# Two blocks of two layers on one core: the norm between the blocks moved behind the first index products, and the first block's attention maxima moved ahead of two rotations

## The chip, the cores and the metric

One core of a Trainium2 chip runs the whole program. The metric is the device time in microseconds (us) of one execution, the median of several. The engines are TensorE (PE in the rows; PEld is its weight load), VectorE (DVE), ScalarE (ACT), GpSimd (POOL) and SyncE (SP), which each work through a list of their own in order and wait for one another on semaphores.

## What is computed

512 tokens of width 1024 pass through two layers of a first block and two layers of a second, all in float32:

```
# first block, each of its two layers; then rmsnorm(x, g_final)
h = rmsnorm(x, g_mix);  z = h @ w_in            # q, k, v, retention q/k/v/g, two gates
ya = sliding_window_sink_attention(aq, ak, av, sinks) @ w_a     # window 128, blocks of 128
yb = (norm(chunkwise_retention(rq, rk, rv)) * silu(rg)) @ w_b
x = x + (sigmoid(ga) * ya + sigmoid(gb) * yb) @ w_out
x = x + square(relu(rmsnorm(x, g_mlp) @ w_up)) @ w_down
# second block, each of its two layers
proj = x @ w_in                                  # q, k, v, index q, index k, index weights, ...
dots = einsum('bqhd,bsd->bqhs', q_idx, k_idx) * IDX_DIM ** -0.5
score = einsum('bqhs,bqh->bqs', relu(dots), w_idx * IDX_HEADS ** -0.5)
top_val, top_idx = lax.top_k(score, topk)        # the keys that attention may see
x = layer_norm(DN_ALPHA * x + mixer(...));  x = layer_norm(DN_ALPHA * x + conv_ffn(x))
```

`rmsnorm(x, g)` is x times g times one factor for each token, the inverse root of the mean square over the 1024 features. Between the blocks stands `rmsnorm(x, g_final)`, whose result is the stream x of the second block.

## The kernel before

The stream lies transposed in SBUF: `X[:, k, :]` is feature tile k (128 features on the partitions) by 512 tokens, k from 0 to 7. A float32 product is made from three matmuls: every operand is split into a high part in TensorE's fast format (`x_hi`, `w_hi`, written by ScalarE) and a low part (`x_lo` by VectorE, `w_lo` by GpSimd, value minus high part), and high by high, high by low and low by high are added up in PSUM. `XH` and `XL` hold the parts of the operand.

Weights come in panels of 1 MB, in the order in which they are used. SyncE loads a panel into one of two `RAW` buffers when GpSimd has finished with the panel two before it; ScalarE's `hi(c)` (L1257, two instructions) writes its high part, GpSimd (L349, four instructions) its low part. A few panels, the two index panels of the second block's first layer among them, have high and low buffers of their own (`own_hi`, `own_lo`), so that `hi` doesn't wait for TensorE to be done with an older panel.

The order on each engine is the order of the code. Helpers are generators (`entry`, `gemm_rows`, `norm_squares`) that are advanced by hand inside other loops with `run(work, n)`, n steps at a time. `T.after`, `A.after`, `V.after` are the waits of TensorE, ScalarE and VectorE for named events, `done` names one.

Entry to a layer of the first block. TensorE multiplies `x * g_mix` without the token factor (`u_hi`, `u_lo`, VectorE L1997) while the squares of x are summed on VectorE (L1961, events `n1_acc`); `token_sums` (L660) reduces the sum over the partitions, ScalarE takes the root (L1537, `token_root`), VectorE the reciprocal (L1988, `n1_inverse`), and `spread` (L715) writes the factor to all partitions of PSUM bank 5. The factor goes into the rotation table (L2283) and, with `scale_again` (L2010, L1939), into a second pair XH/XL for the rest of the products. In layer 0 `start_clock` (L667) runs dummy matmuls ahead of the first products.

Attention of the first block (L740 on TensorE, L2062 on VectorE) runs in 8 steps of two pairs of heads; steps 0 and 1 use q tiles 0, 1 and 2, 3. TensorE's order is `scores(0)`, one piece of filler product (12 matmuls), `scores(1)`, filler, `scores(2)`. `scores(i)` (L746) writes PSUM banks 4 and 5 and waits for `roped 1` or `roped 3`, the rotation of its q tiles, and, from i = 1 on, for `s_read` of step i - 1, which is VectorE's `maxima(i - 1)` (L2055, a masked read of the scores with their minimum, L2060). VectorE's order ahead of it is `scale_again`, the rotations (`rope`, four instructions L1944 to L1950) of tiles 4, 1, 2, 3 (in layer 1: tiles 0, 1, 4 before `scale_again`, tiles 2 and 3 behind it), `maxima(0)`, `maxima(1)`. ScalarE loads the retention's rotation table into `ROT` once `roped 3` is there, and then starts the exponentials.

The feed-forward ends with eight tiles m added to X by VectorE (L2236); events `ffn_out k`. In its last part ScalarE calls `run(beside, 5)`, five steps of the next layer's entry, and then `hi` of the next panel, or of the next two where they have buffers of their own; VectorE runs one step of its own entry behind each addition from m = 2 on.

Between the blocks `inverse_deviation` (L719) on TensorE waits for the last squares, sums them, waits for the factor and spreads it, with dummy matmuls (`keep_clock`, L674) in the gaps; `norm` writes X scaled, `x_hi` and `x_lo`; then `gemm_two` multiplies the two index panels, 8 rows k of 12 matmuls of 384 columns into banks 0 to 3, and `gemm` the panel `misc` (index key, index weights).

Of the kernel before, what the change touches and what calls it, by code (L numbers as in the profile page):

```python
# [15 lines left out]
F32 = mybir.dt.float32  # L16
# [210 lines left out]
def program(nc, stream, x_in, consts_in, rot_in, vec_in, wgate_in, pos_in, out, marks):  # L227
    ctx = ExitStack()
    with ctx:
# [282 lines left out]
        def _(pe):  # L512
# [80 lines left out]
            def gemm_two(n, banks, ready, high_ready, name, columns):  # L593
# [7 lines left out]
                for k in range(KD):  # L601
# [5 lines left out]
                    for j, b in enumerate(banks):  # L607
                        c, p = (k * 2 + j % 2) * P, n + j // 2
                        mm = pe.matmul(PS[:, b, columns], high(p)[:, c:c + P], XL[:, k, columns], start=False, stop=(k == KD - 1))
                        if k == KD - 1:  # L610
                            T.done(mm, *name(j))
                marks[("panel", n)] = marks[("panel", n + 1)] = marks[name(3)]
# [105 lines left out]

            def inverse_deviation(bank, t, l, which):  # L719

                T.after((t, l, which + "_acc", KD - 2), bank_reader[bank], own=False)
                token_columns(TMP[:, 2, :], bank, P, True, False)
                T.after((t, l, which + "_sq", KD - 1), own=False)
                T.done(token_columns(TMP[:, (KD - 1) % 2, :], bank, P, False), t, l, which + "_ms")
                bank_reader[bank] = (t, l, which + "_root")
                keep_clock(bank + 1, 1)
                spread(bank + 1, (t, l, which + "_inverse"), (t, l, which + "_spread"))
                bank_reader[bank + 1] = (t, l, which + "_scaled", KD - 1)
                keep_clock(bank, 2)
# [241 lines left out]
            start_clock(5)  # L971
            for l in range(DEPTH):
# [11 lines left out]
                run(keys, 2)  # L984
# [98 lines left out]
            inverse_deviation(4, "f", 0, "n1")  # L1083

            for l in range(DEPTH):
# [4 lines left out]
                gemm_two(w["iq"], banks, h_ready, lambda k: (t, l, "x_hi", k), lambda m: (t, l, "q", 8 + m), columns_b(8))  # L1090
# [150 lines left out]
        def _(act):  # L1241
# [55 lines left out]
            def attention(pairs, l, t, fillers):  # L1297
# [31 lines left out]
                exponentials(0)  # L1329
                exponentials(1)  # L1330
# [202 lines left out]
            def token_root(bank, ready, name):  # L1533

                A.after(ready)
                sums = PS[:, bank, 0:S:P] if name[0] == "f" else PS[:, bank, 0:NB]
                A.done(act.activation(ST[:, 100:104], sums, ACT.Sqrt, scale=1.0 / D, bias=ST[:, 96:97]), *name)  # L1537

            def norm(t, l, which, squared, bank, second_panel, to_x=False):
# [1018 lines left out]
```

How the kernel before makes its waits and increments, by code:

```python
    def after(self, *names, own=True):  # L205
        need = {}
        for name in names:
            if name is None or (name not in self.marks and not self.marks.get("complete")):
                continue
            who, n = self.marks[name]
            need[who] = max(need.get(who, 0), n)
        if own:
            need[self.name] = self.n
        for who, n in need.items():
            if n > 0:
                self.eng.wait_ge(self.sems[who], n)
# [65 lines left out]
        def const_dma(eng, dst, src, name):  # L283
            if n_consts[0]:
                eng.wait_ge(const_loaded, 16 * n_consts[0])
            eng.dma_start(dst, src).then_inc(const_loaded, 16)
            n_consts[0] += 1
            marks[name] = ("const", 16 * n_consts[0])
# [27 lines left out]
        @block.sync  # L317
# [6 lines left out]
            sp.dma_start(RAW[:, 1, :], stream[1:2, :, :].rearrange("o p n -> p (o n)")).then_inc(raw_full[1], 16)
            with sp.Fori(1, NPANELS // 2) as i:
                for s in range(2):
                    sp.wait_ge(lo_ready, 2 * i + s + 1)
                    sp.dma_start(RAW[:, s, :], stream[bass.ds(2 * i + s, 1), :, :].rearrange("o p n -> p (o n)"))\
                        .then_inc(raw_full[s], 16)
            for k in range(KD):
                sp.wait_ge(sems["act"], marks.get(("b", DEPTH - 1, "ln2_x", k), ("act", 1))[1])
                sp.dma_start(out.rearrange("(k p) s -> p k s", p=P)[:, k, :], X[:, k, :]).then_inc(stored, 16)
            sp.wait_ge(stored, 16 * KD)
```

## Time and profile before

| | before |
|---|---|
| median of 3 executions | 3340.94 us (3340.58 to 3341.14) |
| the profiled execution: own time, span | 3339.35 us, 3337.5 us |
| TensorE matmul busy | 3301.5 us, 99% |
| VectorE, ScalarE, GpSimd busy | 1567.9, 1370.2, 1470.4 us |
| HBM read | 294.74 MB, 89 GB/s over the span |

The span is the stretch from the first to the last instruction of the profiled execution; 1.85 us of its own time lie around it. Times in the text below are us from the start of the span. "Busy" of a matmul is the modelled time from start to end; neighbours overlap, so the pace of TensorE is read from the distance of starts.

### The profile page before, as it was taken

How to read it: one execution, taken by the hardware profiler on the slowest of the kernel's cores; microseconds unless marked ns; L12 is line 12 of the kernel's file. 1: busy time of each engine (PE TensorE's matmuls, PEld its weight loads, DVE VectorE, ACT ScalarE, POOL GpSimd, SP SyncE). 2: the span in 40 equal slices, each digit the busy share in tenths (PEclk: the TensorE clock that was granted, in tenths of full speed). 3: DMA queues.
4: the chain of work that ended last, by engine and by line, in shares of the span. 5: the costliest groups of instructions: out<-in, count | busy, mean ns of one | idle time of the engine just before them, and what ended most of it. 6: DMA issues, size and time to landing. Idle time of an engine off the chain costs nothing. (4 is left out here: it accounts for less than half of the span.)

```text
span 3337.5 us, 45362 instructions
## 1 busy us (share of the span) xinstructions
PE 3301.5 (99%) x16670; PEld 2748.5 (82%) x16670; DVE 1567.9 (47%) x2488; ACT 1370.2 (41%) x1989; POOL 1470.4 (44%) x1102
## 2 busy tenths in 40 slices
PE   9999999999999999999999999999999999999998
PEld 7888888888788888888878888888887788888887
DVE  7523332226514442224973446544488625464445
ACT  5535332224635342223364453333343635443333
POOL 4433544445343444445433345445544233445453
PEclk9999999999999999999999999999999999999999
DMA  4222222222222322222211222222222121222221
GB/s 153 89 73 86 89 103 95 94 101 95 77 76 76 103 100 100 89 101 106 88 66 66 73 92 99 84 95 101 101 81 87 64 76 68 97 85 92 101 98 66
DMA packets 44014, 299.02 MB, mean 90 GB/s; under 512 B 4816, under 2 KB 5456, under 8 KB 8784
## 3 DMA queue, kind: packets, MB, share of 16 engines
q1 hardware_dynamic: 41696, 291.52, 24.5%
q10 hardware_dynamic: 2160, 5.33, 0.5%
q8 instruction: 107, 1.75, 0.2%
q14 instruction: 51, 0.42, 0.0%
HBM read 294.74 MB, written 2.10 MB: 89 GB/s over the span
## 5 line engine op out<-in xcount | busy, mean ns | idle before, releaser
L349 POOL TENSOR_TENSOR w_lo<-w_raw,w_hi 128x512 fp32r<-128x512 f32 x1024 | 1364.6, 1365 | 1778.2 <-ACT w_hi L1257 1778.2
L526 PE MATMUL ps<-x_hi,w_hi 128*128 128x512 f32 x2296 | 907.2, 395 | 3.1 <-DVE arena L2195 2.2
L528 PE MATMUL ps<-x_hi,w_lo 128*128 128x512 f32 x2296 | 894.8, 390 | 0.0
L527 PE MATMUL ps<-x_lo,w_hi 128*128 128x512 f32 x2296 | 894.1, 389 | 0.0
L1257 ACT ACTIVATE w_hi<-w_raw 128x1024 fp32r<-128x1024 f32 x516 | 515.9, 1049 | 463.0 <-PE ps L528 339.4
L526 PEld LDWEIGHTS ps<-x_hi,w_hi 128*128 128x128 f32 x2296 | 431.5, 188 | 100.3 <-issue 6.4
L528 PEld LDWEIGHTS ps<-x_hi,w_lo 128*128 128x128 f32 x2296 | 431.2, 188 | 91.2
L527 PEld LDWEIGHTS ps<-x_lo,w_hi 128*128 128x128 f32 x2296 | 431.6, 188 | 89.0 <-issue 2.2
L526 PE MATMUL ps<-y_hi,w_hi 128*128 128x512 f32 x1056 | 411.9, 390 | 2.2 <-issue 1.9
L528 PE MATMUL ps<-y_hi,w_lo 128*128 128x512 f32 x1056 | 410.9, 389 | 0.0
L527 PE MATMUL ps<-y_lo,w_hi 128*128 128x512 f32 x1056 | 410.8, 389 | 0.0
L2236 DVE TENSOR_TENSOR x<-x,ps 128x512 f32<-128x512 f32 x272 | 182.2, 684 | 255.5 <-PE ps L528 255.3
L2195 DVE SCALAR_TENSOR_TENSOR arena<-ps,vec,arena 128x511 f32<-128x511 f32 (+1 forms) x176 | 131.5, 749 | 300.4 <-ACT arena L1467 290.1
L526 PEld LDWEIGHTS ps<-y_hi,w_hi 128*128 128x128 f32 x1056 | 198.2, 188 | 45.1 <-issue 4.2
L527 PEld LDWEIGHTS ps<-y_lo,w_hi 128*128 128x128 f32 x1056 | 198.2, 188 | 41.5 <-issue 0.5
L528 PEld LDWEIGHTS ps<-y_hi,w_lo 128*128 128x128 f32 x1056 | 198.2, 188 | 41.3
L632 PE MATMUL ps<-w_hi,x_hi 128*128 128x256 f32 x768 | 222.2, 289 | 1.2 <-POOL w_lo L349 1.2
L633 PE MATMUL ps<-w_hi,x_lo 128*128 128x256 f32 x768 | 217.1, 283 | 0.0
L634 PE MATMUL ps<-w_lo,x_hi 128*128 128x256 f32 x768 | 217.1, 283 | 0.0
L1273 ACT ACTIVATE arena<-ps 128x512 f32<-128x512 f32 x136 | 81.3, 598 | 315.8 <-PE ps L528 240.6
L1467 ACT ACTIVATE arena<-ps,vec 128x512 f32<-128x512 f32 x88 | 68.4, 779 | 277.4 <-PE ps L528 277.4
L2206 DVE SCALAR_TENSOR_TENSOR arena<-ps,tmp 128x512 f32<-128x512 f32 x64 | 44.0, 691 | 238.5 <-PE ps L528 224.9
(269 smaller groups left out, 4178.7 us busy)
## 6 DMA issues: line engine op xcount, KB each, us to landing
w_raw<-stream SPq DMA_DIRECT2D x274, 1024.0 KB, 4.8
x<-x_t SPq DMA_DIRECT2D x4, 512.0 KB, 8.1
rotary<-rot ACTq DMA_DIRECT2D x4, 512.0 KB, 4.0
y_t<-x SPq DMA_DIRECT2D x8, 256.0 KB, 2.1
ct<-consts ACTq DMA_DIRECT2D x2, 770.0 KB, 4.4
arena<-pos ACTq DMA_DIRECT2D x2, 256.0 KB, 2.6
w_gate<-w_gate_in ACTq DMA_DIRECT2D x2, 256.0 KB, 2.8
vec<-vectors ACTq DMA_DIRECT2D x4, 116.0 KB, 2.0
```

Source lines behind the costliest of these rows:

```text
L349: ins = nc.gpsimd.tensor_tensor(low(c)[:, o:o + S], RAW[:, c % 2, o:o + S], high(c)[:, o:o + S].bitcast(F32), ALU.subtract)
L526: pe.matmul(ps, wh, xh, start=(k == 0), stop=False)
L527: pe.matmul(ps, wh, xl, start=False, stop=False)
L528: return pe.matmul(ps, wl, xh, start=False, stop=last)
L632: pe.matmul(ps, xh, wh, start=(k == 0), stop=False)
L633: pe.matmul(ps, xl, wh, start=False, stop=False)
L634: mm = pe.matmul(ps, xh, wl, start=False, stop=(k == KD - 1))
L1257: act.activation(wh[:, o:o + 2 * S], RAW[:, s, o:o + 2 * S], ACT.Copy)\
L1273: A.done(act.activation(dst, bank_of(*name), func, **kw), *(("read",) + name))
L1467: act.activation(AR[:, j, :], PS[:, j, :], ACT.Identity, scale=VEC[:, l % 2, bass.ds(tap, 1)], bias=VEC[:, l % 2, bass.ds(bias, 1)]).then_ ...
L2195: ins = dve.scalar_tensor_tensor(AR[:, j, tap:S], PS[:, j, 0:n], wv, AR[:, j, tap:S], ALU.mult, ALU.add)
L2236: dve.tensor_tensor(X[:, m, :], X[:, m, :], PS[:, 4 + m % 4, :], ALU.add).then_inc(down_added, 1)
```

## The change

Four edits.

1. `start_clock(5)` becomes `start_clock(8)`: eight dummy matmuls at the start in place of five.
2. In the entry to a layer of the first block TensorE runs one row of the key/value product between `token_sums` and `spread`, in place of two.
3. Attention of the first block: `maxima(0)` stands ahead of the rotations of q tiles 2 and 3, which stood ahead of it; on ScalarE the load of the second rotation table stands behind the first exponentials.
4. Between the blocks: the stream times `g_final`, without the token factor, is split (`u_hi`, `u_lo`, in a third entry generator, `last_entry`, which the last feed-forward advances), and the two index panels are multiplied with it. `token_sums` stands behind row 1, `spread` behind row 2. Index scores are relu of a product, so the positive factor of a query token can be put on the index weights: one more VectorE instruction there. The scaled stream X and its parts are written during rows 3 to 7 (`scale_stream`), each `x_hi k` when row k has been read. `inverse_deviation` and its dummy matmuls are gone.

```diff
-            start_clock(5)
+            start_clock(8)
...
-                run(keys, 2)
+                run(keys)
                 spread(5, (t, l, "n1_inverse"), (t, l, "n1_spread"))
...
-            inverse_deviation(4, "f", 0, "n1")
-
...
+                    index = gemm_two_rows(w["iq"], banks, lambda k: ("f", 0, "u_lo", k), lambda k: ("f", 0, "u_hi", k),
+                                          lambda m: (t, l, "q", 8 + m), columns_b(8), lambda k: ("f", 0, "u_read", k))
+                    run(index, 2)
+                    token_sums(TMP[:, 2, :], 4, ("f", 0, "n1_acc", KD - 1), ("f", 0, "n1_ms"))
+                    bank_reader[4] = ("f", 0, "n1_root")
+                    run(index)
+                    spread(5, ("f", 0, "n1_inverse"), ("f", 0, "n1_spread"))
...
# ScalarE
                 exponentials(0)
+                for _ in behind_first:
+                    pass
                 exponentials(1)
...
+            def last_entry():
+
+                x_ready = lambda k: ("a", DEPTH - 1, "ffn_out", k)
+                squared = norm_squares("f", 0, "n1", x_ready)
+                for k in range(KD):
+                    A.after(x_ready(k), "vec%d" % (DEPTH - 1))
+                    g = VB["g_final"] + k
+                    A.done(act.activation(XH[:, k, :], X[:, k, :], ACT.Copy, scale=VEC[:, 1, g:g + 1]), "f", 0, "u_hi", k)
+                    yield
+                    if k < 6:
+                        run(squared)
+                        yield
                 for _ in squared:
                     pass
                 warm_root()
-                token_root(bank, (t, l, which + "_ms"), (t, l, which + "_root"))
+                token_root(4, ("f", 0, "n1_ms"), ("f", 0, "n1_root"))
...
# VectorE
+            def last_entry():
+
+                adding = square_sums("f", 0, "n1")
+                for k in range(KD):
+                    g = VB["g_final"] + k
+                    V.after(("f", 0, "u_hi", k), "vec%d" % (DEPTH - 1), own=False)
+                    V.done(dve.scalar_tensor_tensor(XL[:, k, :], X[:, k, :], VEC[:, 1, g:g + 1],
+                                                    XH[:, k, :].bitcast(F32), ALU.mult, ALU.subtract), "f", 0, "u_lo", k)
+                    if k:
+                        run(adding)
+                    yield
...
                 maxima(0)
+                for _ in behind_first:
+                    pass
                 maxima(1)
...
-                for j in [j for j in (4, 1, 2, 3) if j not in early]:
+                for j in [j for j in (4, 1) if j not in early]:
                     rope(AR[:, j, :], SWAP_A, (t, l, "roped", j), [("read", t, l, "q", j)])
+
+                def last_ropes():
+                    for j in (2, 3):
+                        rope(AR[:, j, :], SWAP_A, (t, l, "roped", j), [("read", t, l, "q", j)])
+                        yield
...
+                if l == 0:
+                    V.done(dve.tensor_tensor(iw, iw, ST[:, 104:108].unsqueeze(2).broadcast_to([P, NB, 8]), ALU.mult))
```

How the edits stand in the lists of the engines. First VectorE at the start of the attention in layer 1 of the first block, before: the last of `scale_again`, the rotations of tiles 2 and 3 (the second is left out, it has the same four rows), then `maxima(0)`.

```order
L1939 TENSOR_TENSOR x_lo<-tmp,x_hi 128x512 x2
L1944 STREAM_SHUFFLE tmp<-arena 128x512
L1946 TENSOR_TENSOR tmp<-tmp,rotary 128x512
L1948 TENSOR_TENSOR arena<-arena,rotary 128x512
L1950 TENSOR_TENSOR arena<-arena,tmp 128x512
...
L2055 ISA tmp,stats<-ct,ps,stats 128x128
L2055 ISA stats 128x1
```

The same place in the changed kernel (its lines are numbered differently: 1939 is now 1961, 1944 to 1950 are 1966 to 1972, 2055 and 2060 are 2077 and 2082).

```order
L1961 TENSOR_TENSOR x_lo<-tmp,x_hi 128x512 x2
L2077 ISA tmp,stats<-ct,ps,stats 128x128
L2077 ISA stats 128x1
...
L2082 TENSOR_TENSOR stats<-stats 128x4
L1966 STREAM_SHUFFLE tmp<-arena 128x512
L1968 TENSOR_TENSOR tmp<-tmp,rotary 128x512
L1970 TENSOR_TENSOR arena<-arena,rotary 128x512
L1972 TENSOR_TENSOR arena<-arena,tmp 128x512
...
L2077 ISA tmp,stats<-ct,ps,stats 128x128
```

The first masked read of the scores has moved past both rotations; nothing else on VectorE has moved there. In layer 0 it is the same, with the rotations of tiles 4 and 1 ahead of `maxima(0)`.

Second, ScalarE at the end of the last feed-forward of the first block, before: high parts of the feed-forward's last panels and of the two index panels, then the eight squares and the root.

```order
L1257 ACTIVATE w_hi<-w_raw 128x1024 x6
L1257 ACTIVATE own_hi0<-w_raw 128x1024 x2
L1257 ACTIVATE own_hi1<-w_raw 128x1024 x2
L1282 ACTIVATE tmp<-x 128x512 x8
L1531 ACTIVATE stats<-stats 128x1
L1537 ACTIVATE stats<-ps,stats 128x4
```

The same place in the changed kernel (L1559 writes `u_hi`, L1289 a square).

```order
L1264 ACTIVATE w_hi<-w_raw 128x1024 x6
L1559 ACTIVATE x_hi<-x,vec 128x512
L1289 ACTIVATE tmp<-x 128x512
L1559 ACTIVATE x_hi<-x,vec 128x512
L1289 ACTIVATE tmp<-x 128x512
L1559 ACTIVATE x_hi<-x,vec 128x512
L1264 ACTIVATE own_hi0<-w_raw 128x1024 x2
L1264 ACTIVATE own_hi1<-w_raw 128x1024 x2
L1289 ACTIVATE tmp<-x 128x512
```

The high parts of both index panels have moved behind three `u_hi` and two squares.

Third, TensorE between the blocks, before: the last matmul of the feed-forward, the sums, dummies, spread, dummies, and the first index row.

```order
L528 MATMUL ps<-y_hi,w_lo 128x512
L679 MATMUL ps<-ct,tmp 128x128 x8
L674 MATMUL ps<-ct 128x256 x2
L715 MATMUL ps<-ct,stats 128x128 x4
L674 MATMUL ps<-ct 128x256 x4
L531 MATMUL ps<-x_hi,own_hi0 128x384
```

In the changed kernel the first index row follows the feed-forward's last matmul; this is the stretch from the end of index row 1 to the start of row 3 (row 2 is cut to its first two rows and its last).

```order
L613 MATMUL ps<-x_lo,own_hi1 128x384 x2
L668 MATMUL ps<-ct,tmp 128x1 x4
L531 MATMUL ps<-x_hi,own_hi0 128x384
L532 MATMUL ps<-x_hi,own_lo0 128x384
...
L613 MATMUL ps<-x_lo,own_hi1 128x384 x2
L723 MATMUL ps<-ct,stats 128x128 x4
L531 MATMUL ps<-x_hi,own_hi0 128x384
```

The sums and the spread now stand between rows of the index product, and the dummies are gone.

## Rows read from the trace of the kernel before

**Rows 1.** The page: busy time, and the clock granted to TensorE in 40 slices

```profile
PE 3301.5 (99%) x16670; PEld 2748.5 (82%) x16670; DVE 1567.9 (47%) x2488; ACT 1370.2 (41%) x1989; POOL 1470.4 (44%) x1102
PEclk9999999999999999999999999999999999999999
```

**Rows 2.** Waits of TensorE over the span: total, times, longest

```profile
PE ps L746 <- DVE stats L2055: 5.0, 2, 3.0
```

**Rows 3.** Timeline of TensorE at the start: start, duration, instruction, [idle before <- released by]

```profile
1.35 4.64 PE L667 MATMUL ps<-tmp 128*128 128x256 f32 x10 [1.35 <-DVE tmp L1935]
8.91 0.77 PE L531 MATMUL ps<-x_hi,w_hi 128*128 128x512 f32 x1 [2.92 <-ACT x_hi L1566]
...
14.15 0.39 PE L531 MATMUL ps<-x_hi,w_hi 128*128 128x512 f32 x1
...
28.25 1.05 PE L660 MATMUL ps<-ct,tmp 128*128 128x1 f32 x8 [0.29 <-DVE tmp L1961]
```

**Rows 4.** Timeline of VectorE at the start: six of the seven sums of squares

```profile
19.84 8.35 DVE L1961 TENSOR_TENSOR tmp<-tmp,scratch 128x512 f32<-128x512 f32 x6
```

**Rows 5.** Timeline of TensorE, start of the attention in layer 0

```profile
63.43 0.71 PE L746 MATMUL ps<-arena 64*128 64x128 f32 x8
...
70.05 0.81 PE L746 MATMUL ps<-arena 64*128 64x128 f32 x8 [2.95 <-DVE stats L2055]
```

**Rows 6.** Timeline of VectorE there: tile 1 from its shuffle, tiles 2 and 3, maxima

```profile
56.53 0.73 DVE L1944 STREAM_SHUFFLE tmp<-arena 128x512 f32<-128x512 f32 x1
...
59.57 0.75 DVE L1944 STREAM_SHUFFLE tmp<-arena 128x512 f32<-128x512 f32 x1
60.36 1.67 DVE L1946 TENSOR_TENSOR tmp<-tmp,rotary 128x512 f32<-128x512 f32 x1
...
67.87 0.69 DVE L1950 TENSOR_TENSOR arena<-arena,tmp 128x512 f32<-128x512 f32 x1
68.74 0.35 DVE L2055 CUSTOM_DVE_ANT_0 tmp<-ct,ps,stats 128x128 f32<-128x128 f32 x1 [0.18 <-DVE arena L1950]
...
69.94 0.16 DVE L2060 TENSOR_TENSOR stats<-stats 128x4 f32<-128x4 f32 x1
```

**Rows 7.** Timeline of GpSimd there: one panel's low part, and layer 1's

```profile
60.18 6.38 POOL L349 TENSOR_TENSOR w_lo<-w_raw,w_hi 128x512 fp32r<-128x512 f32 x4 [5.06 <-ACT w_hi L1257]
...
829.47 5.62 POOL L349 TENSOR_TENSOR w_lo<-w_raw,w_hi 128x512 fp32r<-128x512 f32 x4 [3.26 <-ACT w_hi L1257]
```

**Rows 8.** Timeline of TensorE, start of the attention in layer 1

```profile
827.27 0.71 PE L746 MATMUL ps<-arena 64*128 64x128 f32 x8
...
832.99 1.12 PE L746 MATMUL ps<-arena 64*128 64x128 f32 x8 [2.06 <-DVE stats L2055]
```

**Rows 9.** Timeline of VectorE there: the end of `scale_again`

```profile
820.96 2.40 DVE L1939 TENSOR_TENSOR x_lo<-tmp,x_hi 128x512 fp32r<-128x512 f32 x2 [0.21 <-ACT x_hi L1277]
```

**Rows 10.** Timeline of TensorE between the blocks: last matmul, first index row, `misc`

```profile
1550.28 0.39 PE L528 MATMUL ps<-y_hi,w_lo 128*128 128x512 f32 x1
...
1557.47 0.41 PE L531 MATMUL ps<-x_hi,own_hi 128*128 128x384 f32 x1
...
1574.46 0.47 PE L526 MATMUL ps<-x_hi,w_hi 128*128 128x512 f32 x1
```

**Rows 11.** Timeline of ScalarE: the high part of the second index panel

```profile
1540.11 2.01 ACT L1257 ACTIVATE own_hi<-w_raw 128x1024 fp32r<-128x1024 f32 x2 [7.21 <-DMA w_raw<-stream]
```

**Rows 12.** Timelines at the end of layer 0's feed-forward: ScalarE, GpSimd, TensorE, VectorE

```profile
768.61 0.72 ACT L1566 ACTIVATE x_hi<-x,vec 128x512 fp32r<-128x512 f32 x1 [1.27 <-DVE x L2236]
...
771.80 6.44 POOL L349 TENSOR_TENSOR w_lo<-w_raw,w_hi 128x512 fp32r<-128x512 f32 x4 [5.83 <-ACT w_hi L1257]
...
781.06 0.39 PE L528 MATMUL ps<-y_hi,w_lo 128*128 128x512 f32 x1
781.28 0.39 PE L531 MATMUL ps<-x_hi,w_hi 128*128 128x512 f32 x1
...
787.94 1.59 DVE L1961 TENSOR_TENSOR tmp<-tmp 128x512 f32<-128x512 f32 x1
```

More of the change, by code:

```diff
@@ L591, in gemm_rows, with gemm_two, gemm_two_rows @@
                 marks[("panel", n)] = marks[name(ms - 1)]
-            def gemm_two(n, banks, ready, high_ready, name, columns):
+            def gemm_two(*args):
+                for _ in gemm_two_rows(*args):
+                    pass
+            def gemm_two_rows(n, banks, ready, high_ready, name, columns, read=None):
                 for p in range(2):
@@ L611, in gemm_two @@
                             T.done(mm, *name(j))
+                        elif read and j == 3:
+                            T.done(mm, *read(k))
+                    if k < KD - 1:
+                        yield
                 marks[("panel", n)] = marks[("panel", n + 1)] = marks[name(3)]
@@ L717, in spread @@
                 T.done(mm, *name)
[L719 to L729, printed above, removed]
             def attention(pairs, l, t, fillers, ahead=0):
@@ L1591, in _ @@
             hi(0)
-            entries = [entry(l) for l in range(DEPTH)]
+            entries = [entry(l) for l in range(DEPTH)] + [last_entry()]
             for l in range(DEPTH):
@@ L1956, in sums @@
             def sums(src, ready, name):
-                for k in range(1, KD - 1 if name[0] == "f" else KD):
+                for k in range(1, KD):
                     a = src(0) if k == 1 else TMP[:, 2, :]
@@ L2003, in entry, with scale_stream @@
                     pass
+            def last_entry():
+                adding = square_sums("f", 0, "n1")
+                for k in range(KD):
+                    g = VB["g_final"] + k
[4 more added lines that the diff above has]
+                        run(adding)
+                    yield
+                for _ in adding:
+                    pass
+            def scale_stream(gain):
+                for k in range(KD + 1):
+                    if k < KD:
+                        V.after(("f", 0, "n1_spread"), own=False)
+                        V.done(dve.scalar_tensor_tensor(X[:, k, :], X[:, k, :], VEC[:, 1, gain + k:gain + k + 1],
+                                                        PS[:, 5, :], ALU.mult, ALU.mult), "f", 0, "n1_scaled", k)
+                    if k:
+                        j = k - 1
+                        lo(XL[:, j, :], X[:, j, :], XH[:, j, :], [("b", 0, "x_hi", j)], ("b", 0, "x_lo", j), own=False)
             def scale_again(t, l, gain):
@@ L2268, in ffn @@
                     pass
-            entries = [entry(l) for l in range(DEPTH)]
+            entries = [entry(l) for l in range(DEPTH)] + [last_entry()]
             for l in range(DEPTH):
```

77 lines of the change are left out of this document (34 added, 43 removed).

## The prediction

> **What bounds the kernel now.** I read the page first. TensorE is busy for 3301.5 of 3337.5 us, no other engine for half of that [rows 1]. So an edit counts only where it changes how long TensorE idles or what it computes. The largest group of TensorE's waits is `scores` waiting for VectorE's maxima, 5.0 us in two waits, one in each layer of the first block [rows 2]. Then I read the timelines at the four edited places and followed each wait back to what was late. The start: dummies from 1.35, an idle stretch of 2.92, the first product at 8.91. The 12 matmuls up to 14.15 take 5.24 us, 0.44 each, the pace of the lower clock (1.2 GHz), though the page's granted clock reads full; from there on they start every 0.23 [rows 1, 3, 12]. Between the blocks: 7.0 us from the start that the next matmul could have had, 1550.28 + 0.23 = 1550.51, to 1557.47 [rows 10].
>
> **Edit 1, eight dummies.** Ten records (two for each dummy) take 4.64 us [rows 3], so sixteen end near 8.6, ahead of 8.91: no delay. The gain may be that the clock is up when the products start: at most 5.24 - 12 x 0.23 = 2.5 us. But `token_sums` already waits for VectorE: 0.29 us idle, started at 28.25 when the last sum of squares was done, 19.84 + 8.35 = 28.19 [rows 3, 4]. VectorE and ScalarE don't get faster by a faster TensorE, so TensorE comes 2.5 us earlier to the same wait. Value 0, bounds 0 and -0.3.
>
> **Edit 2, spread one row earlier.** The same matmuls in another order: 0 on TensorE. VectorE gets the factor one row (1.4 us) earlier; what it does with that is in edit 3. Value 0.
>
> **Edit 3, maxima first.** In layer 0 VectorE is done with tile 1 at 56.53 + 3.04 = 59.57 and has used the time until `scores(0)` ends at 63.43 + 0.71 = 64.14 to rotate tiles 2 and 3; it comes to `maxima(0)` at 68.74 [rows 5, 6]. In the changed list `maxima(0)` is in front of those rotations, so VectorE stands still until 64.14 and begins them behind it. `scores(1)` needs both, the maxima (its banks) and `roped 3` (its q tiles), and comes later:
> - `maxima(0)` from 64.2 takes 69.94 + 0.16 - 68.74 = 1.4, to 65.6.
> - A rotation alone takes 3.0 (56.53 to 59.57) [rows 6]. GpSimd's panel began at 60.18 and took 6.38 beside a busy VectorE [rows 7]; with VectorE idle it is over by 66, so both rotations go undisturbed: 65.6 + 6.1 = 71.7.
> - `scores(1)` at 71.75, against 70.05 [rows 5]: +1.7. Bounds: +1.5, and +2.7 if one instruction of a rotation is slowed (1.67 for 0.69 [rows 6]).
>
> In layer 1 `scores(0)` ends at 827.98 and `scores(1)` starts at 832.99 [rows 8]. `scale_again` is over at 823.36 [rows 9], so the 4.6 us up to 828 are lost to VectorE. Maxima to 829.4. The rotations now meet GpSimd's next panel, which starts at 829.47 [rows 7]. That is the situation of tiles 2 and 3 in layer 0 before, where a panel started 0.6 us behind the first shuffle: those two rotations took from 59.57 to 67.87 + 0.69 = 68.56, 9.0 us [rows 6, 7]. So `roped 3` at 838.4, `scores(1)` at 838.5: +5.5. Bounds: +2.6 if nothing contends (6.1 in place of 9.0), +6.2 if one more instruction is slowed. Behind `scores(1)` the exponentials of step 0 are long done, so nothing else grows; the table load behind `roped 3` moves by as much as TensorE's own work. The maxima are not what is late here: VectorE's rotations are, and the edit starts them later.
>
> **The restart.** TensorE would idle 71.75 - 67.10 = 4.7 us in layer 0 and 838.5 - 830.9 = 7.6 us in layer 1. The longest idle stretch in the trace that began at the full pace is 2.95, and matmuls behind it are at full pace at once; the start, behind dummies and 2.92 idle, costs up to 2.5 [rows 3, 5]. So the price of each restart lies between 0 and 2.5. The gap of 4.7 is nearer to the row without cost: 0. The gap of 7.6 is 2.6 times that row, and I take 2.4, nearly the row of the start. The Trainium skill ("TensorE: Matmul & The Clock Gate", part 1 on the HAM clock gate) says that the slow state is the default, returns after a stretch of idleness, and is left only by sustained activity. By that rule the restart in layer 1 is slow; by the row of 2.95 alone it would be free and the sum below 2.4 lower. No row here shows a fall in mid-kernel.
>
> **Edit 4, between the blocks.** The best case is that index rows start at 1550.51 and run through: 8 rows of 17.0/8 = 2.12 us [rows 10], plus sums and spread of 0.9 each (1.05 with the overlap of eight such records [rows 3]), to 1569.3 against 1574.46: -5.2. Two things stand against it.
> - Weights. ScalarE makes the index panels' high parts behind the third `u_hi`. The end of layer 0's feed-forward has the same list: its third `u_hi` ends at 769.33, TensorE's last matmul starts at 781.06 [rows 12]. Shifted by 1550.28 - 781.06 = 769.22 that is 1538.6. The first panel's low part so starts at 1539.7, a panel takes 6.44 us beside VectorE's entry work [rows 12], the two 12.9: ready at 1552.6. The second raw panel is there at 1540.1 [rows 11], early enough. TensorE waits 2.1 us where it waited for nothing.
> - The sum of squares. In the same stretch of layer 0 it ends at 787.94 + 1.59 = 789.53 [rows 12], shifted 1558.75. There ScalarE splits a weight panel before the last squares, here not, but GpSimd is in VectorE's way for longer; I take 1558.4. Rows 0 and 1 end at 1552.6 + 4.2 = 1556.8, so TensorE waits 1.6 more.
> Then 1558.4 + 0.9 + 2.1 (row 2; root and reciprocal take under 1 us beside it) + 0.9 + 5 x 2.12 = 1572.9 against 1574.46: -1.6. Bounds -5.2 and 0.
> What follows is covered: `x_hi k` and `x_lo k` trail the rows by under 1.5 us and `misc` reads k 0.7 us apart; the extra instruction on 32 index weights has several tiles of products ahead of the first dots. Cover gone, it would cost 0.2.
>
> The Trainium skill ("SBUF — State Buffer", section "SBUF: two separate sides") says that a VectorE instruction with two SBUF inputs and a GpSimd instruction exclude each other for their whole length. The rows agree for VectorE, whose 0.69 becomes 1.67, and less for GpSimd, whose panels stay between 5.62 and 6.44 us [rows 6, 7, 12]. If each of the eight GpSimd instructions (5.62/4 = 1.4) had to let one VectorE instruction of 0.7 pass, the index panels would take 16.8 us, TensorE would start at 1556.5 and `misc` at 1575.2: this edit would cost 0.7 where I have -1.6.
>
> **Sum.** 0 + 0 + 1.7 + 5.5 + 2.4 - 1.6 = +8.0 us: the profiled execution's own 3339.35 becomes 3347.3. It lay 1.6 under the median of the three; on the median of 3340.9 the forecast is 3348.9 us. A measurement of this kernel tells about 0.2%, 6.7 us, from no change; the forecast is just beyond it.
>
> **Rivals.**
> - *Only the longer gap restarts slowly* (forecast): 3348.9, between 3346.9 and 3351. Chance 0.40.
> - *Both restarts at full pace.* For it: the 2.95 us idle without a trace. Against: 7.6 us is far more. 5.6 over before: 3346.5. Chance 0.27.
> - *Both slow.* Another 2.4: 3351.3. Chance 0.15.
> - *The gap between the blocks closes in full, restarts at full pace.* For it: the same arrangement at the end of layer 0 cost TensorE no wait. Against: there no index panels hung behind the entry. 1.7 + 5.5 - 5.2 = +2.0: 3342.9. Chance 0.10.
> - *The other side: maxima first frees the second scores.* Both waits [rows 2] vanish, -5.0, and with -1.6 between the blocks 3334.3, on the edge of what is faster. It decides if tiles 2 and 3 are rotated before TensorE ends its filler piece, at 67.1 and 830.9. With `maxima(0)` behind `scores(0)`, 3.0 and 2.9 us earlier, even one rotation hardly fits. Chance 0.08.
>
> **Numbers.** The range leaves out the last rival and the ends of the second and third by their bounds: 3341.5 to 3352. Slower by over 0.2% (over 3347.6): most of the forecast's case, 0.35, all of "both slow", 0.15, and a little of the second, 0.02: 0.52. Faster: most of the last rival, 0.06. Within: the rest, 0.42.
>
> **What would show it.** VectorE idle ahead of its first masked read for 4 us or more in both layers, and the wait of `scores(1)` grown from 2.95 and 2.06 to 4.7 and 7.6. Matmuls 0.43 apart behind the gap in layer 1. No gain at `token_sums` in layer 0: 2.8 us idle there. Between the blocks GpSimd's second own panel ends near 1552.6 (plus what came before), as a wait of TensorE's first index row, and another at the sums; `misc` starts 1.6 us earlier relative to the feed-forward's last matmul. I am wrong if `roped 3` isn't late, that is if rotations aren't what `scores(1)` waits for.

## The result and the profile after

The changed kernel takes 3355.59 us (median of 6 runs, 3354.38 to 3356.91), the kernel before 3341.11 (6 runs beside it, 3340.58 to 3341.23). The ratio is 1.0042, with a 95% interval of 1.003 to 1.0053: slower by 14.5 us, where 8 were forecast, and outside the range. The profiled execution took 3356.59 us, its span is 3354.7, 17.2 more than before; it lies 1.0 above its median, where the profiled one of before lay 1.6 below.

The page of the changed kernel; these two lines answer to [rows 1]. TensorE is busy 4.1 us more (3305.6 for 3301.5) and idles the rest of the 17.2; the granted clock still reads full in every slice, but a slice is 84 us long:

```profile
PE 3305.6 (99%) x16656; PEld 2751.4 (82%) x16656; DVE 1578.9 (47%) x2498; ACT 1375.6 (41%) x1997; POOL 1470.1 (44%) x1102
...
PEclk9999999999999999999999999999999999999999
```

TensorE's waits over the span, to be held against [rows 2]: engine, line, what is waited for, then total, times and longest in us.

```profile
PE ps L742 <- DVE arena L1972: 11.7, 2, 7.0
PE ps L526 <- issue: 6.9, 3, 4.7
PE ps L668 <- DVE tmp L1983: 2.4, 2, 1.4
...
PE ps L531 <- POOL own_lo L349: 2.3, 1, 2.3
```

The two waits of `scores(1)` (L742) were 5.0 us and are 11.7. "issue" was 1.9 and is 6.9: one new wait of 4.7 that the profile puts down to nothing. The wait for the index panels (own_lo) is the forecast one.

TensorE at the start of the attention in layer 0, then in layer 1 (start, duration, instruction, idle before):

```profile
73.11 1.32 PE L742 MATMUL ps<-arena 64*128 64x128 f32 x8 [4.69 <-DVE arena L1972]
...
74.94 0.63 PE L527 MATMUL ps<-x_lo,w_hi 128*128 128x512 f32 x1
75.37 0.63 PE L528 MATMUL ps<-x_hi,w_lo 128*128 128x512 f32 x1
...
843.12 1.32 PE L742 MATMUL ps<-arena 64*128 64x128 f32 x8 [7.00 <-DVE arena L1972]
...
844.96 0.63 PE L527 MATMUL ps<-x_lo,w_hi 128*128 128x512 f32 x1
845.38 0.63 PE L528 MATMUL ps<-x_hi,w_lo 128*128 128x512 f32 x1
```

The granted clock of the same trace over short stretches (start:end, length, busy time and instructions of PE, PEld, DVE, ACT and POOL, then the granted clock as a share of full speed, the DMA engines' busy share, GB/s):

```profile
72.00:73.00 1.00, 0.00 (x0) 0.00 (x0) 0.93 (x2) 0.00 (x0) 0.00 (x0) 0.50 0.00 0
78.00:80.00 2.00, 2.00 (x13) 1.21 (x11) 0.00 (x0) 0.76 (x2) 0.00 (x0) 1.00 0.00 0
844.00:849.00 5.00, 5.00 (x16) 3.81 (x14) 2.43 (x13) 2.18 (x9) 0.00 (x0) 0.50 0.53 206
```

Starts 0.43 apart behind both gaps and a granted clock of 0.50: the lower clock (1.2 GHz). In layer 0 it had fallen before the gap was over. From `scores(1)` to `scores(2)`, the same work, it takes 5.87 us in layer 0, where it took 3.67, and 6.51 in layer 1, where it took 5.25.

That 5.25 holds something which the prediction overlooked. The timeline of the kernel **before**, behind the wait of 2.06 us in [rows 8]:

```profile
834.04 0.79 PE L526 MATMUL ps<-x_hi,w_hi 128*128 128x512 f32 x1
834.63 0.63 PE L527 MATMUL ps<-x_lo,w_hi 128*128 128x512 f32 x1
835.06 0.63 PE L528 MATMUL ps<-x_hi,w_lo 128*128 128x512 f32 x1
...
836.75 0.40 PE L526 MATMUL ps<-x_hi,w_hi 128*128 128x512 f32 x1
836.99 0.40 PE L527 MATMUL ps<-x_lo,w_hi 128*128 128x512 f32 x1
```

Its granted clock there, in the columns used above:

```profile
834.00:836.00 2.00, 2.00 (x6) 1.57 (x6) 1.32 (x9) 1.89 (x8) 1.09 (x1) 0.50 0.23 92
```

The kernel before already restarts slowly here, six starts 0.43 apart; its `scores(1)` row itself says so (1.12 for eight matmuls that take 0.81 in layer 0).

VectorE in layer 1 of the changed kernel: it idles until `scores(0)` is done, takes the maxima, and then rotates tiles 2 and 3 up to 842.97, beside GpSimd's panel (834.65 to 840.97):

```profile
833.22 0.35 DVE L2077 CUSTOM_DVE_ANT_0 tmp<-ct,ps,stats 128x128 f32<-128x128 f32 x1 [4.67 <-PE ps L742]
...
834.72 0.76 DVE L1966 STREAM_SHUFFLE tmp<-arena 128x512 f32<-128x512 f32 x1
835.51 0.99 DVE L1968 TENSOR_TENSOR tmp<-tmp,rotary 128x512 f32<-128x512 f32 x1
836.54 1.64 DVE L1970 TENSOR_TENSOR arena<-arena,rotary 128x512 f32<-128x512 f32 x1
838.21 1.63 DVE L1972 TENSOR_TENSOR arena<-arena,tmp 128x512 f32<-128x512 f32 x1
...
839.98 0.73 DVE L1966 STREAM_SHUFFLE tmp<-arena 128x512 f32<-128x512 f32 x1
...
842.28 0.69 DVE L1972 TENSOR_TENSOR arena<-arena,tmp 128x512 f32<-128x512 f32 x1
```

Between the blocks, TensorE and then ScalarE:

```profile
1561.67 0.39 PE L528 MATMUL ps<-y_hi,w_lo 128*128 128x512 f32 x1
1564.35 0.41 PE L531 MATMUL ps<-x_hi,own_hi 128*128 128x384 f32 x1 [2.30 <-POOL own_lo L349]
...
1569.72 1.05 PE L668 MATMUL ps<-ct,tmp 128*128 128x1 f32 x8 [0.96 <-DVE tmp L1983]
...
1588.99 0.77 PE L526 MATMUL ps<-x_hi,w_hi 128*128 128x512 f32 x1 [4.71 <-issue]
1589.56 0.63 PE L527 MATMUL ps<-x_lo,w_hi 128*128 128x512 f32 x1
1589.98 0.63 PE L528 MATMUL ps<-x_hi,w_lo 128*128 128x512 f32 x1
```

```profile
1584.31 0.63 ACT L1284 ACTIVATE x_hi<-x 128x512 fp32r<-128x512 f32 x1 [1.91 <-PE ps L613]
1586.00 0.63 ACT L1284 ACTIVATE x_hi<-x 128x512 fp32r<-128x512 f32 x1 [1.06 <-DVE x L2046]
1586.00 0.34 ACTq L287 DMA_DIRECT2D vec<-vectors  x1
1587.96 0.33 ACTq L287 DMA_DIRECT2D w_gate<-w_gate_in  x1
1588.40 1.66 ACT L1771 ACTIVATE arena<-ps 128x384 f32<-128x384 f32 x3 [1.78 <-DMA vec<-vectors]
```

The last index row ends at 1584.3. `misc`, which should follow at once, starts at 1588.99. ScalarE's first copy of an index tile starts at 1588.40 and takes a third of 1.66: it ends at 1588.95. Ahead of it stand `x_hi 6`, `x_hi 7` and the issue of two loads, the second of which waits until the first has landed. In the kernel before, ScalarE stood ready and the copies began at 1573.87, during the last row's last matmuls.

Stretch by stretch, in the two profiled executions, the 17.2 us are: 1.3 up to `scores(0)` of layer 0; 1.7 and 4.9 for the later `scores(1)`; 2.2 and 1.3 for the slow restarts behind them; 3.1 from the last matmul of the feed-forward to `misc` (27.32 for 24.18); 2.1 for the slow restart of `misc`; 0.5 in the rest. (Before rounding, the two terms at `misc` are 3.14 and 2.13, 5.3 together: the transposes of the index weights behind it start 40.43 us behind the feed-forward's last matmul, where they started 35.16 behind it.)

### The profile page after: what moved, and what is told of

Its sections match the earlier page's. It is cut to its first block and busy times, and to the rows that moved or that the text cites. A ratio compares the mean times of both kernels' runs of the same rounds, so it can differ in the third digit from the quotient of the medians.

```text
span 3354.7 us, 45371 instructions
## 1 busy us (share of the span) xinstructions
PE 3305.6 (99%) x16656; PEld 2751.4 (82%) x16656; DVE 1578.9 (47%) x2498; ACT 1375.6 (41%) x1997; POOL 1470.1 (44%) x1102
```

## The experiments

All ran beside the kernel before, whose median was 3341.2, 3341.7, 3341.2 and 3341.35 us in the four groups. Its single times run from 3339.2 to 3345.0.

### Edit 3 alone

```diff
-    for j in [j for j in (4, 1, 2, 3) if j not in early]:
+    for j in [j for j in (4, 1) if j not in early]:
         rope(...)
...
     maxima(0)
+    for _ in behind_first:
+        pass
     maxima(1)
```

> The kernel before with edit 3 alone (first maxima and the second table's load ahead of the rotations of tiles 2 and 3). Theory (the rows of the changed kernel read stretch by stretch): scores(1) comes 1.7 us later in layer 0 and 4.9 in layer 1, and each gap before it brings TensorE down to the lower clock, 2.2 and 1.3 us: +10.1, about 3351.2 us, with matmuls 0.43 us apart behind both gaps. Rival: the slow stretch in layer 0 needs the other edits too (in the changed kernel the clock had fallen once already near 30 us), so that only the gap of layer 1 restarts slowly: +7.9, 3349.0. Second rival, both restarts at full pace: +6.6, 3347.7.

Measured: 3349.87 us, ratio 1.0025 (1.0015 to 1.0035), 8.7 more. Its trace has the same gaps, 4.69 and 7.00, and TensorE restarts slowly behind both. `scores(1)` comes 1.7 and 4.9 us later behind `scores(0)` than in the kernel before. From `scores(1)` to `scores(2)` it takes 6.59 in layer 0 (2.9 more) and 5.32 in layer 1 (0.1 more). The time lies between the theory's and its first rival's, but the trace rules the rival out: the gap of layer 0 restarts slowly without the other edits. The theory's 1.3 for layer 1 was chance; most of that cost is paid before as well.

### Edit 4 alone

```diff
-            inverse_deviation(4, "f", 0, "n1")
...
+                    run(index, 2)
+                    token_sums(TMP[:, 2, :], 4, ("f", 0, "n1_acc", KD - 1), ("f", 0, "n1_ms"))
+                    run(index)
+                    spread(5, ("f", 0, "n1_inverse"), ("f", 0, "n1_spread"))
```

> The kernel before with edit 4 alone (index rows from the unscaled stream between the blocks). Theory: what the changed kernel's rows show there belongs to this edit: a wait of 2.3 us for the index panels' low parts, one of 1 us at the sums, and one of 4.7 us ahead of the misc panel, which restarts slowly (2.1 us): +3.1 up to misc's first matmul, +5.2 behind it, 3346.3 us. Rival (the forecast's sum): the 4.7 us ahead of misc are brought on by the other edits, which shift the transfers against TensorE; alone the edit gives -1.6, 3339.5 us.

Measured: 3346.6 us, ratio 1.0017 (1.0007 to 1.0026), 5.4 more. The gap ahead of `misc` is 4.75, with 14 slow matmuls behind it. So the gap comes from this edit and not from the others.

### Edits 1 and 2, each alone

```diff
-            start_clock(5)
+            start_clock(8)
```

> The kernel before with edit 1 alone (eight dummies at the start). Theory: the clock is up before the first product, the rows of products then outrun VectorE and idle between rows, and the clock falls behind the wait for the token sums near 30 us: matmuls 0.43 apart for some 3 us there, +1.3 us, 3342.4. Rival (the forecast's term): nothing, 3341.1 us, because the fall near 30 us comes from the spread that edit 2 moves; then the matmuls behind it are 0.23 apart.

```diff
-                run(keys, 2)
+                run(keys)
                 spread(5, (t, l, "n1_inverse"), (t, l, "n1_spread"))
```

> The kernel before with edit 2 alone (layer 0's spread one row of products earlier, in the entry to both layers). Theory, as in the forecast: the same products in another order, 0: 3341.4 us. Rival: the spread then waits for VectorE's reciprocal, and TensorE falls to the lower clock near 30 us as it did in the changed kernel's profile: +1.3, 3342.7.

Measured: eight dummies 3341.74 us, ratio 1.0003 (0.9993 to 1.0012); the earlier spread 3341.12, ratio 1.0 (0.9991 to 1.001). The profile of the first has no slow stretch near 30 us, though TensorE idles 1.44 there, against 1.42 in the changed kernel, which has one. Of the two accounts of that stretch in the expectation neither holds. It comes in some executions and not in others, and neither edit brings it: six of the experiments' profiles have one, with a granted clock of 0.50 from some point between 29.0 and 30.3 us on, and none of those kernels has either edit. Both terms of 0 stand.

The four edits alone give 8.7 + 5.4 + 0.6 - 0.1 = 14.6; together they gave 14.5.

### The gaps of the changed kernel filled

```diff
                 scores(0)
                 run(fillers)
+                if t == "a":
+                    T.after(*bank_reader[6:8], own=False)
+                    for _ in range((9, 14)[l]):
+                        pe.matmul(PS[:, 6, 0:2 * P], CT[:, 128:256], CT[:, 0:256], start=True, stop=True)
                 scores(1)
```

> The changed kernel with matmuls on constants in the gap ahead of scores(1) of the first block (9 of 256 columns in layer 0, 14 in layer 1, about 0.47 us each: 4.2 and 6.6 us, a little under the gaps of 4.7 and 7.0); their results are not used. Theory: the slow stretch behind each gap is the price of TensorE's idleness, so scores(1) starts where it did and the matmuls behind it are 0.23 apart: -2.2 and -1.3, 3352.1 us. Rival: the slow stretch comes from something else at that place, such as VectorE's and GpSimd's work beside it; then nothing changes, 3355.6 us.

Measured: 3351.92 us, ratio to the kernel before 1.0032 (1.0019 to 1.0044), 3.7 less than the changed kernel. Its TensorE in layer 1:

```profile
832.43 6.20 PE L772 MATMUL ps<-ct 128*128 128x256 f32 x28
839.61 0.82 PE L742 MATMUL ps<-arena 64*128 64x128 f32 x8 [0.97 <-DVE arena L1976]
840.36 0.50 PE L526 MATMUL ps<-x_hi,w_hi 128*128 128x512 f32 x1
840.70 0.39 PE L527 MATMUL ps<-x_lo,w_hi 128*128 128x512 f32 x1
```

The gap of 7.0 is 28 records of the added matmuls and 0.97 of idleness; behind it starts are 0.23 to 0.34 apart. `scores(1)` comes 10.68 us behind `scores(0)`, as without the filling (10.66). So the delay and the slow restart are two costs: the first is VectorE's, the second is the price of idleness. From `scores(1)` to `scores(2)` it takes 3.69 and 3.70 us, where it took 5.87 and 6.51, so this trace has 5.0 us back; the medians have 3.7.

### Maxima between the two rotations

```diff
-    for j in [j for j in (4, 1) if j not in early]:
+    for j in [j for j in (4, 1, 2) if j not in early]:
...
-                    for j in (2, 3):
+                    for j in (3,):
```

> The kernel before with the first maxima between the rotations of tiles 2 and 3 (in edit 3 they stand ahead of both). Theory: what costs in edit 3 is that VectorE stands idle for scores(0); with one rotation ahead of the maxima it hardly does. Layer 0: rotation 2 ends near 64.2, maxima to 65.7, rotation 3 to 69.5, scores(1) 0.5 us earlier than 70.05; layer 1: 0.5 later than 832.99. Together 0: 3341.2 us. Rival (the place of the rotations behind the maxima is what costs, each of them): half of edit 3's waits, +3.3, 3344.5 us.

Measured: 3344.15 us, ratio 1.0008 (0.9998 to 1.0017), 2.5 more: nearer to the rival. `scores(1)` comes 6.70 us behind `scores(0)` in layer 0 (before 6.62) and 7.53 in layer 1 (before 5.72). With one rotation ahead, layer 0 costs nothing (0.1) and layer 1 1.8. The gap there grows from 2.06 to 3.86 and the restart behind it takes 6.20 to `scores(2)`, 0.95 more than before (5.25).

### Why misc waits: another bank, and another place for the load

```diff
+                if l == 0:
+                    kept, tile[0] = tile[0], 7
+                    ring[0] = 8
                 gemm(w["misc"], KD, 1, XH, XL, h_ready, lambda m: (t, l, "q", 12))
+                if l == 0:
+                    tile[0] = kept + 1
+                    ring[0] = 4
```

> The kernel before with edit 4 alone, and the misc panel's products in PSUM bank 7 in place of bank 0. Theory: the 4.7 us that TensorE idles ahead of misc are a wait for bank 0, which ScalarE copies out late; bank 7 is free, so misc follows the last index row at once and at full pace: 4.7 + 2.1 to 2.9 less than edit 4 alone (3346.6), about 3339.5 us. Rival: misc waits for its data (the second panel's low part or the high and low parts of the stream); then the gap stays, 3346.6 us.

```diff
-                const_dma(act, WG[:, :], wgate_in[l], ("w_gate", l))
+                if l:
+                    const_dma(act, WG[:, :], wgate_in[l], ("w_gate", l))
...
+                    if i == 1 and l == 0:
+                        const_dma(act, WG[:, :], wgate_in[l], ("w_gate", l))
```

> The kernel before with edit 4 alone, and the load of w_gate issued behind ScalarE's four copies of index tiles in place of ahead of them. Theory: ScalarE reads bank 0 late because it stands behind x_hi 7 and then 1.8 us behind the load, whose issue waits for the landing of the vectors; without that the copies start 1.8 us earlier and the gap ahead of misc is 2.9 us in place of 4.7: 3344.8 us, or down to 3342.5 if the shorter gap restarts at full pace. Rival: the load is not in the way (the copies wait for TensorE or for the data), nothing changes: 3346.6 us.

In bank 7 `misc` follows the last row without a gap, 22.8 us behind the feed-forward's last matmul in place of 27.7, and the index weights' transposes come 7.8 us earlier behind that matmul (33.82 for 41.59; at 1585.93 for 1593.37, 7.4, by the two spans' own times). So the wait was for the bank. With the load moved the gap is 3.01, 1.7 less; the profile there names GpSimd, but `misc` starts at 1580.69, when ScalarE's first copy ends (1580.10 and a quarter of 2.25), and it restarts slowly.

But the times are 3345.79 (1.0012, 1.0002 to 1.0021) and 3345.02 (1.0008, 0.9999 to 1.0018). That is 4.1 and 3.4 more than the kernel before beside them, where edit 4 alone had 5.4 more: 1.3 and 2.1 gained. Of bank 7's 7.8 us at the transposes 4.2 are left at the sixth dots (84.17 us behind the feed-forward for 88.39), by waits at the dots, and 1.3 in the medians; what takes the rest is not shown. The theory was right about the wait and wrong about its worth. TensorE in the kernel with bank 7, at the dots:

```profile
1611.89 0.92 PE L1120 MATMUL ps<-arena 64*128 64x384 f32 x4 [0.69 <-ACT tmp L1762]
...
1622.17 0.92 PE L1120 MATMUL ps<-arena 64*128 64x384 f32 x4 [1.08 <-ACT tmp L1762]
```

### What takes it back: the repaired edit 4

The first index panel's high part ahead of the first `u_hi`, then also the copies of tiles 8 and 9 between `x_hi 6` and `x_hi 7`:

```diff
+                        if ff + per * groups in own_place:
+                            hi(ff + per * groups)
+                            run(beside, 5)
...
                 split_hi(XH[:, k, :], X[:, k, :], ...)
+                if k == 6:
+                    for j in (8, 9):
+                        A.after(("b", 0, "q", j))
+                        A.done(act.activation(AR[:, j, columns_b(j)], ...), "read", "b", 0, "q", j)
```

> As the kernel with bank 7, and ScalarE makes the high part of the first index panel ahead of the first u_hi in place of behind the third; the second stays behind the third. Theory: GpSimd's first panel starts some 4 us earlier, the low parts are ready before TensorE ends the feed-forward, and the wait of 2.3 us ahead of the first index row goes; the sum of squares then is late by more, but is itself freed of GpSimd earlier: 0.5 to 2 us less than with bank 7 alone, 3338.2 us. Rival: the wait only moves to the token sums, 3339.5 us.

> Edit 4 alone with misc in bank 7 and the first index panel early, and besides ScalarE copies index tiles 8 and 9 between x_hi 6 and x_hi 7 and loads w_gate behind the copies. Theory: with bank 7 alone the gain of 7.4 us at misc was given back at the dots, because VectorE began to rotate the index tiles 5.3 us later than in the kernel before, for want of ScalarE's copies; now it begins right behind x_lo 7, 1.5 us sooner, so about 1.5 of the 3 us of waits at the dots go: 1.5 less than the kernel with bank 7 and the early panel (3344.2), 3342.7 us, still not below the kernel before. Rival: the dots wait for something else (the index weights' extra instruction), no change: 3344.2.

Measured: 3344.19 us (1.0009, 0.9999 to 1.0018) and 3343.13 (1.0005, 0.9996 to 1.0014). In both the first index row starts 0.23 behind the last matmul, without a wait. In the second the transposes come 32.87 us behind the feed-forward, 2.3 less than before (35.16), but the sixth dots 83.63 behind it, 1.7 more than before (81.96). VectorE between the rows' end and the dots, in the kernel before and then in the repaired one (the first index tile's shuffle, in the repaired kernel the index weights' extra instruction, the shuffle of q tile 3):

```profile
1574.59 0.59 DVE L1944 STREAM_SHUFFLE scratch<-arena 128x384 f32<-128x384 f32 x1
...
1606.98 0.74 DVE L1944 STREAM_SHUFFLE scratch<-arena 128x512 f32<-128x512 f32 x1
```

```profile
1575.25 0.59 DVE L1988 STREAM_SHUFFLE scratch<-arena 128x384 f32<-128x384 f32 x1
...
1591.65 0.87 DVE L2417 TENSOR_TENSOR stats<-stats 128x32 f32<-128x32 f32 x1
...
1608.47 0.73 DVE L1988 STREAM_SHUFFLE scratch<-arena 128x512 f32<-128x512 f32 x1
```

VectorE works without a break between these in either kernel. Behind the feed-forward's last matmul it begins 0.7 us later (25.04 for 24.31) and does 0.87 more; so it is 1.6 late at the last of them, and the sixth dots are 1.7 late.

That the two numbers agree is partly chance. In this one profile the granted clock fell twice in the stretch, during the index rows and at the dots. The last kernel of the experiments, called the combined one here (the repaired edit 4, matmuls in the gaps, eight dummies), has the same order in this stretch, and in its profile the clock did not fall there. Two stretches of the repaired kernel, then two of the combined one:

```profile
1557.00:1560.00 3.00, 3.00 (x11) 3.00 (x11) 0.18 (x1) 2.15 (x3) 1.23 (x1) 0.50 0.00 0
1619.00:1621.00 2.00, 2.00 (x7) 1.16 (x4) 1.81 (x3) 0.00 (x0) 0.00 (x0) 0.50 0.84 352
```

```profile
1548.00:1580.00 32.00, 30.74 (x168) 28.30 (x167) 26.22 (x40) 17.49 (x29) 14.12 (x10) 1.00 0.30 106
1600.00:1632.00 32.00, 29.99 (x129) 19.92 (x128) 29.19 (x42) 12.45 (x16) 12.69 (x8) 1.00 0.19 62
```

In the combined kernel VectorE begins 23.89 behind the feed-forward, the transposes come 31.15 behind it, 4.0 less than before, and the sixth dots 80.36, 1.6 less than before. TensorE waits at the third and fourth dots as in the repaired kernel's profile (0.15, 0.48 and 1.08, beside 0.16, 0.52 and 1.08). So between the transposes and the sixth dots 2.4 us are given back without a fall of the clock and 4.0 with one. The slower rotation of the third index tile, which the expectation for the repaired kernel with less work counts on (5.4 us beside GpSimd's panel, where it took 2.5), doesn't matter: in the kernel before it is the fourth and the sixth rotation that meet a panel, and from the first shuffle to that of q tile 3 the two kernels differ by 0.83 us (33.22 for 32.39), which is the extra instruction.

Whether VectorE is what the dots wait for was the question of two more kernels, which leave out two of its rotations:

```diff
-                for j in range(8, 13):
+                for j in (8, 9, 12) if l == 0 else range(8, 13):
                     rope_b(j)
```

> Control: the kernel before, leaving out VectorE's rotation of index tiles 10 and 11 in the first layer of the second block (the dots take them unrotated), about 5 us less for VectorE there. Theory: in the kernel before TensorE waits for nothing at the first six dots, so VectorE's time there is covered: 3341.2 us. Rival (VectorE already sets the end of that stage in the kernel before, by the top-k behind it): 2 to 5 less, 3337.5.

> The repaired edit 4 (3343.1 us), leaving out the same two rotations. Theory: misc and the index weights come 2.4 us earlier there than in the kernel before, relative to its own start of the rows, and 4 us are given back between the index weights and the dots of the third row block, because VectorE, which gets the index tiles late and rotates the third beside GpSimd's panel (4.8 us for 2.5), weighs the dots late. With 5 to 7 us less of its work the waits at the dots go: 4 less, 3339.1 us, 2 below the kernel before. Rival: the dots wait for ScalarE's copies or a panel; then the gain stays below 1: 3342.5.

Measured: 3340.79 (1.0, 0.999 to 1.0009) and 3339.17 (0.9991, 0.9981 to 1.0001). The same cut is worth 0.6, within the noise, in the kernel before, and 4.0 in the repaired one. In its trace the transposes and the sixth dots both come 3.95 us earlier behind the feed-forward than before: nothing is given back. It is VectorE that the dots wait for. The waits are worth 2.4 of the 4.0: against the combined kernel, whose profile has no fall of the clock here either, the sixth dots come 2.35 us earlier (78.01 for 80.36). The rest is not explained; fewer falls of the clock may be part of it. The third and fourth dots in the repaired kernel, and there with the cut:

```profile
1607.99 0.92 PE L1120 MATMUL ps<-arena 64*128 64x384 f32 x4
1609.07 0.92 PE L1120 MATMUL ps<-arena 64*128 64x384 f32 x4 [0.16 <-ACT tmp L1772]
...
1616.16 0.92 PE L1120 MATMUL ps<-arena 64*128 64x384 f32 x4 [0.52 <-ACT tmp L1772]
1618.16 1.53 PE L1120 MATMUL ps<-arena 64*128 64x384 f32 x4 [1.08 <-ACT tmp L1772]
```

```profile
1607.46 1.56 PE L1120 MATMUL ps<-arena 64*128 64x384 f32 x8
1614.61 1.56 PE L1120 MATMUL ps<-arena 64*128 64x384 f32 x8
```

### Fillings in the gaps of the kernel before

The same lines as above with `(5, 3)[l]`: alone, and with the repaired edit 4 and eight dummies at the start.

> The kernel before with matmuls on constants in its own gaps ahead of scores(1): 5 of 256 columns in layer 0 (gap 2.95), 3 in layer 1 (gap 2.06); their results are not used. Theory: gaps of 2 to 3 us already bring TensorE to the lower clock, in layer 1 nearly always (1.2 us: six matmuls 0.43 apart), in layer 0 in about one execution of four (some 2 us); filled, both are gone: 1.2 to 1.7 less, 3339.8 us. Rival: gaps below 3 us cost nothing and the slow stretch has another cause, or the added matmuls take what they give: 3341.4.

> The repaired edit 4, the matmuls on constants ahead of both scores(1), and eight dummies at the start; the maxima as in the kernel before. Theory: the parts add up, -1.5 for the filled gaps, +1.3 for the repaired edit 4, 0 for the start: about 3341.2 us. Rival (each of these saves time where TensorE waited, so that they only add where nothing behind is late): above 3342.

Measured: 3340.15 us (0.9995, 0.9986 to 1.0004) and 3340.20 (0.9996, 0.9987 to 1.0005). Both medians are 1.0 below the kernel before, neither surely below it; by the medians of its parts (+1.95 for the repaired edit 4, -1.03 for the fillings) the second would be 0.9 above it, so the two didn't cost more together than apart. In the traces the stretch behind the filled gap of layer 1 takes 3.70 and 3.72 us in place of 5.25, so the slow restart is gone; the rest of an execution scatters by more. No tried version that does the whole work is measurably faster than the kernel before.

## Why the prediction was wrong

The direction was right, the size was not. Point by point:

- **Edits 1 and 2, terms of 0.** Right: +0.6 and -0.1, both within their intervals. Of the 2.8 us of idleness named as a sign at `token_sums`, 1.4 came; part of it lies earlier, in waits of a few tenths within the rows of products (0.32 for `x_lo` in the first).
- **Edit 3, the delays, +1.7 and +5.5.** Right in mechanism: VectorE idles 4.74 and 4.67 us ahead of the first masked reads. They measured 1.7 and 4.9. The rotations in layer 1 took 8.3 us (834.72 to 842.97) where I took 9.0 from layer 0's. The rival in which the maxima free the second scores fell.
- **The restart in layer 0: "The gap of 4.7 is nearer to the row without cost: 0."** Wrong. It cost 2.2 here and 2.9 in edit 3 alone, the second above my bound of 2.5, and filling both gaps gave 3.7 back. The step under it, "No row here shows a fall in mid-kernel", was a misreading: in the kernel before the matmuls from 832.99 on, behind 2.06 us of idleness, are at the lower clock, and the granted clock of that trace reads 0.50 from 834 to 836. I had read the pace behind one of its two waits only. The Trainium skill ("TensorE: Matmul & The Clock Gate", part 1) had the better rule: the slow state returns after idleness, and by it both restarts are slow, my third case. The traces agree for every gap from 3.86 us up (8 of 8).
- **The restart in layer 1, +2.4.** Mis-sized: against the full pace (3.70 us to `scores(2)`) the restart costs 2.8 here, near the 2.4, but the kernel before pays 1.5 of that already (5.25), so the edit added 1.3 in one profile and 0.1 in another.
- **Edit 4, up to the sums.** Right in size: GpSimd's second panel ended at 1564.15, which is 1552.8 on the clock of before (-11.39), against 1552.6; the waits were 2.3 and 0.96 for 2.1 and 1.6. The rows ended at 1584.28, which is 1572.9 on that clock, the forecast's figure to the tenth. The eight GpSimd instructions took 13.2 us, near my 12.9. The 16.8 counted too much: it added 0.7 to 1.4, a mean that already held such delays. In this trace the first of the eight takes 1.29 and the others, each beside a VectorE instruction with two inputs in SBUF, 1.70 to 1.76. So each gave way by some 0.45, and the 13.2 says nothing against the exclusion.
- **Edit 4, "What follows is covered: `x_hi k` and `x_lo k` trail the rows by under 1.5 us".** This is the step that failed. I asked only when `misc`'s data would be there, not when its bank would be. ScalarE used to finish `x_hi 7` at 1568.26, 5.6 us before the first copy, and stood waiting to copy. In the changed order it starts `x_hi 7` 1.7 us behind the rows' end, then issues two loads, then copies. The "under 1.5 us" was wrong too: `x_hi 4` starts at 1581.26, 3.2 us behind its row, because the high part of the second `misc` panel (1579.37 to 1581.36) stands ahead of it. Together with a slow restart this made +5.3 (3.14 + 2.13) where I had -1.6.
- **Its best case, -5.2.** Not to be had by TensorE alone. VectorE works without a break from the first index tile to the dots, and TensorE waits for it there: of 4.0 us gained at the transposes in the combined kernel, 1.6 are left at the sixth dots. I had asked nothing of VectorE's chain.

With the terms as measured in the profile (2.2 for 0, 1.3 for 2.4, +5.3 for -1.6, 4.9 for 5.5) the forecast's +8.0 becomes +15.4, near the 14.5 of the medians. The 1.3 near 30 us in the profile and the 0.5 of the rest are scatter by the evidence of the single edits. "Both restarts slow" was given 0.15 at 3351.3; what moved the time out of the range was the wait for the bank with the slow restart behind it: without that 6.9 us (5.3 for -1.6) the medians' 3355.6 would be 3348.7, beside a forecast of 3348.9 in which the other errors happen to cancel.

One thing stays open: why TensorE restarts slowly behind a gap in one execution and at full pace behind a gap of the same length in the next.

## What to carry to other kernels

When an edit makes one engine's queue end later, go through everything behind it in that queue, and ask of each thing that waits for it not only when its data are there, but when its buffer is. Read the pace of the matmuls behind every gap of the kernel at hand, or the granted clock over a stretch of a few microseconds there, before pricing a new one: some are already slow, and a longer gap then adds less. And if a gain on the bounding engine vanishes, cut work from the next engine in both kernels: a cut worth 4.0 us in one and nothing clear of the noise in the other names the engine. Before you explain 1 or 2 us from one profile, look whether the clock fell in it.

## What the runs showed of the hardware

TensorE's clock fell in mid-kernel behind gaps as short as these. The fall shows in two ways that agree: the granted clock over a short stretch reads 0.50, and matmuls of 512 columns start 0.43 us apart in place of 0.23. The page doesn't show it; its slices of 84 us read full in every run. (At the very start of the kernel before the two don't agree: over 10 to 12 us the granted clock reads 1.00 at a pace of 0.44 us. The trace has no record of the clock before 14.12.) Counted in the 16 profiles (before, changed, 14 experiments):

- behind 3.86 to 7.0 us of idleness: always (8 of 8);
- behind 2.95 to 3.04 us ahead of `scores(1)` in layer 0: 3 of 11; behind 3.01 ahead of `misc`: the one time it occurred;
- behind 2.04 to 2.07 us ahead of `scores(1)` in layer 1, which is shorter: 9 of 10;
- behind 1.77 us near 175 us: 1 of 16;
- behind 1.0 to 1.5 us at the token sums near 28 us: 7 of 10.

There were others behind 1.1 to 2.4 us between the blocks and at the dots. The clock fell within the gap or up to 2.2 us after work had resumed. Between `scores(1)` and `scores(2)` a fall cost 1.5 to 2.9 us against the 3.7 at full pace. So length alone doesn't decide it, and the scatter of one kernel's times (3339.2 to 3345.0) is of the size of a few such restarts.
